# A backbone kernel with latent attention, retention and mLSTM: retention strips moved behind weight copies, an adaLN vector computed in two halves, and separate buffers for the second output projection's input

## The reference

```python
for l in range(DEPTH):
    ml = split(silu(c) @ mod_w[l] + mod_b[l], 6)          # g = 0..5: (l, g) is one vector
    h_lat = x * (1 + ml[1]) + ml[0]
    if l == 0:
        # retention: o = sum_j (q_i . k_j) * decay(i - j) * v_j, in both directions, per head
        ret = head_norm(ret_forward + ret_backward) * silu(rg)
        y = concat([attention, ret]) @ ab_w_out
    else:
        y = (sigmoid(og) * head_norm(h_forward + h_backward) * m_norm_g) @ m_w_out
    x = layer_norm(ALPHA * x + ml[2] * y)
    x = layer_norm(ALPHA * x + ml[5] * swiglu(x * (1 + ml[4]) + ml[3]))
```

## Time and profile before

| | |
|---|---|
| median of 3 runs | 1945.5 us (1937.79, 1945.5, 1948.0) |
| profiled execution | 1948.19 us, its span 1946.3 us |
| mean granted TensorE clock | 0.960 of 2.4 GHz |
| busy: PE, DVE, ACT, POOL | 1796.6 us (92%), 691.5 us (36%), 610.6 us (31%), 724.2 us (37%) |
| DMA | 162.82 MB, mean 84 GB/s |

### The profile page before, as it was taken

How to read it: one execution, slowest core, us unless ns; L and a number is a source line. 1 busy time by engine, 2 the same in 40 slices (tenths; PEclk the granted TensorE clock), 3 DMA queues, 4 the chain that set the end, 5 groups by cost and what they waited for, 6 DMA issues and landing times.

```text
span 1946.3 us, 24417 instructions
## 1 busy us (share of the span) xinstructions
PE 1796.6 (92%) x9832; PEld 1436.2 (74%) x9832; DVE 691.5 (36%) x1183; ACT 610.6 (31%) x859; POOL 724.2 (37%) x381
## 2 busy tenths in 40 slices
PE   4999989999899999999999996989775989999996
PEld 2788757555587888888888883777665878888885
DVE  2134235666467411011111136740078661111114
ACT  1522211555335321122212124442324453132224
POOL 0442200166456423222322245433225664445343
PEclk8999989999999999999999997999877999999998
DMA  8421132255312122122221126212100223323221
GB/s 288 118 55 55 55 119 87 87 174 174 109 55 72 48 65 76 54 65 65 65 65 43 48 62 201 64 56 65 54 1 22 87 70 104 108 87 108 87 78 51
DMA packets 210265, 162.82 MB, mean 84 GB/s; under 512 B 17662, under 2 KB 190942, under 8 KB 210182
## 3 DMA queue, kind: packets, MB, share of 16 engines
q1 hardware_dynamic: 207744, 157.77, 27.3%
q10 hardware_dynamic: 2438, 3.90, 0.5%
HBM read 159.55 MB, written 2.10 MB: 83 GB/s over the span
## 4 chain that ended last, share of the span: by engine, by line
PE 78%; DVE 13%; ACT 4%; issue 2%; DMA 2%; POOL 1%; ACTq 0%; SPq 0%; DVEq 0%
PE ps L662 56%; PE ps L650 2%; PE ps L652 2%; PE ps L651 2%; PE ps L818 2%; PE ps L845 2%; PE ps L870 1%; PE ps L759 1%; PE ps L775 1%; DVE xT L1918 1%; DVE xT L1908 1%; DMA ring<-in_mod_w 1%; PE ps L855 1%; PE ps L604 1%; DVE hlo L1687 1%
## 5 line engine op out<-in xcount | busy, mean ns | idle before, releaser
L2267 POOL TENSOR_TENSOR wsplit<-ring,wsplit 128x1024 fp32r<-128x1024 f32 (+1 forms) x136 | 325.5, 2407 | 531.3 <-ACT wsplit L1405 531.2
L662 PE MATMUL ps<-hhi,wsplit 128*128 128x512 f32 (+1 forms) x1920 | 480.4, 358 | 6.4 <-DVE hu L1965 6.3
L662 PEld LDWEIGHTS ps<-hhi,wsplit 128*128 128x128 f32 x1920 | 316.5, 189 | 61.1 <-DVE hu L1965 6.9
L662 PE MATMUL ps<-hlo,wsplit 128*128 128x512 f32 x960 | 289.9, 356 | 0.0
L662 PE MATMUL ps<-uhi,wsplit 128*128 128x512 f32 x1008 | 253.7, 357 | 0.0
L2015 DVE TENSOR_TENSOR hu<-sg,ps 128x768 f32<-128x768 f32 (+1 forms) x40 | 32.9, 821 | 445.6 <-ACT sg L1474 445.6
L1405 ACT ACTIVATE wsplit<-ring 128x1024 fp32r<-128x1024 f32 (+1 forms) x136 | 135.3, 1025 | 176.0 <-PE ps L662 176.0
L662 PEld LDWEIGHTS ps<-uhi,wsplit 128*128 128x128 f32 x1008 | 165.4, 188 | 27.9
L662 PEld LDWEIGHTS ps<-hlo,wsplit 128*128 128x128 f32 x960 | 160.1, 189 | 29.3
L1881 DVE SCALAR_TENSOR_TENSOR xT<-ps,modc,xT 128x512 f32<-128x512 f32 x96 | 60.6, 659 | 280.5 <-PE ps L662 215.6
L2324 POOL TENSOR_SCALAR lnbuf<-lnbuf,den 128x768 f32<-128x768 f32 (+1 forms) x48 | 85.0, 1778 | 180.3 <-DVE den L1839 179.7
(11 more groups left out here) (326 smaller groups left out, 2737.5 us busy)
## 6 DMA issues: line engine op xcount, KB each, us to landing
ring<-in_mod_w SPq DMA_DIRECT2D x96, 512.0 KB, 4.7
ring<-in_ffn_w_in SPq DMA_DIRECT2D x88, 512.0 KB, 3.8
ring<-in_ffn_w_out SPq DMA_DIRECT2D x32, 512.0 KB, 4.0
ring<-in_m_w_in SPq DMA_DIRECT2D x24, 512.0 KB, 3.6
ring<-in_ab_w_in SPq DMA_DIRECT2D x21, 512.0 KB, 3.9
ring<-in_ffn_w_out SPq DMA_DIRECT2D x16, 384.0 KB, 3.5
ring<-in_ab_w_out SPq DMA_DIRECT2D x8, 512.0 KB, 4.6
ring<-in_m_w_out SPq DMA_DIRECT2D x8, 512.0 KB, 3.8
```

The lines of the kernel that those rows point to most:

```text
L662: mm = pe.matmul(dst[:, a:b], w, h[:, a:b], start=st, stop=sp_)
L2267: pool.tensor_tensor(w_part(s, 1)[:, 0:width], ring[:, (NB[f"ffn{l}"] + s) % RING, 0:width], w_part(s, 0)[:, 0:width].bitcast(F32), ALU.su ...
```

## The change

It joins two changes.

*Strips and vector (0,3).* ACT's `strips(h)` is cut in two: the fourth exponential becomes `strips_end(h)`. For strip 0 one weight copy now stands between the two; strip 1 moves from ahead of the copies NF + 3 to NF + 5 to between the last two copies, with its end behind the last. On PE `mod_rows` of (0,3) is cut after four units (RING); `ret_scores(0)` stands between the halves, and `ret_scores(1)` ahead of the columns. On DVE the last rotation stands ahead of strip 1, the row copies of (0,3) behind weighing 0, its columns behind weighing 1, and `strips_args(2)` behind those.

*Own places.* The rounded chunks go to `oT_a` (chunks 0 to 3), `oT_b` (4, 5) and `oT_c` (6, 7), none of which is read or written under live data; the low parts stay in `hlo_out1`. Each chunk gets a half bank of its own. Chunks 0 to 3 are transposed right behind the last `m_values`, each pair behind its own count of `mn_done`, 4 to 7 in `out_projection`.

```diff
@@ buffers @@
-    hb = under(("hb", [P, LT, D], F32))
+    oT_a, hb = under(("oT_a", [P, KD // 2, LAT], F32R), ("hb", [P, LT, D], F32))
+    _, oT_c = under(("oT_c_pad", [P, KD // 2 * LAT], F32), ("oT_c", [P, 2, LAT], F32R))
...
+    oT_b = sb("oT_b", [P, 2, LAT], F32R, at=ph)
...
+    def out_hi(l, c):
+        return hx[:, 0, c, :] if l == 0 else (oT_a[:, c, :] if c < 4 else (oT_b, oT_c)[c // 2 - 2][:, c % 2, :])
+    def oT_bank(l, c):
+        return op_pair(c) if l == 0 else half(c)
@@ PE @@
-        mod_rows(0, 3, PS[2])
+        mod_rows(0, 3, PS[2], 0, RING)
         ret_scores(0)
+        mod_rows(0, 3, PS[2], RING, KD)
+        ret_scores(1)
         mod_columns(0, 3, PS[2])
-        for h in range(1, H_RET):
+        ret_values(0)
+        for h in range(2, H_RET):
             ret_scores(h)
             ret_values(h - 1)
...
-            for c in rg_chunks(l):
-                if l == 1 and c >= 4:
-                    pe.wait_ge(oT_ev, KD * l + c - 3)
-                if l == 1 and c < 2:
-                    pe.wait_ge(mn_done, NP - 1 + c)
-                if l == 1 and c == 2:
+            for c in (rg_chunks(0) if l == 0 else range(4, KD)):
+                if l == 1 and c == 4:
                     pe.wait_ge(m_num, LT * NP)
+                if l == 1 and c % 2 == 0:
+                    pe.wait_ge(mn_done, c // 2 + 1)
...
+                turn_chunk(l, c, source)
             for m in range(KD):
                 if m < 4:
-                    pe.wait_ge(oT_ev, KD * l + 5 + m)
+                    pe.wait_ge(oT_ev, KD * l + (5 + m if l == 0 else 2 * m + 1))
...
             m_values(i + 3)
+            if p == NP:
+                for c in range(4):
+                    if c % 2 == 0:
+                        pe.wait_ge(mn_done, c // 2 + 1)
+                    turn_chunk(1, c, m_source)
@@ ACT @@
         strips(0)
         split_high("in0", NF + 2, wsp_in0[:, 0])
-        strips(1)
+        strips_end(0)
         for i in range(NF + 3, NF + 6):
             split_high("in0", i, wsp_in0[:, 0])
...
-        for i in range(NF + 6, N_IN0):
-            split_high("in0", i, wsp_in0[:, 0])
+        split_high("in0", NF + 6, wsp_in0[:, 0])
+        strips(1)
+        split_high("in0", NF + 7, wsp_in0[:, 0])
+        strips_end(1)
...
         strips(2)
+        strips_end(2)
         ret_copy(0)
         strips(3)
+        strips_end(3)
@@ DVE @@
-        for h in range(2):
-            strips_args(h)
-            strips_mask(h)
-            strips_sum(h)
+        strips_args(0)
+        strips_mask(0)
+        strips_sum(0)
         rope_ret(8)
-        mod_rows(0, 3, PS[2])
+        strips_args(1)
+        strips_mask(1)
+        strips_sum(1)
...
         ret_weigh(0)
+        mod_rows(0, 3, PS[2])
+        ret_weigh(1)
+        mod_columns(0, 3, PS[2])
         strips_args(2)
-        mod_columns(0, 3, PS[2])
-        ret_weigh(1)
```

More of the change, by code:

```diff
@@ L892, in _, with turn_chunk, m_source, out_projection @@
                     mod_columns(*ATT_MODS[q], half(7))
-        def out_projection(l, source, h_hi, h_lo, wsp):
-            for c in rg_chunks(l):
-                if l == 1 and c >= 4:
-                    pe.wait_ge(oT_ev, KD * l + c - 3)
-                if l == 1 and c < 2:
-                    pe.wait_ge(mn_done, NP - 1 + c)
-                if l == 1 and c == 2:
+        def turn_chunk(l, c, source):
+            for t in range(NT[l] // P):
+                mm = pe.transpose(oT_bank(l, c)[:, t * P:(t + 1) * P], source(c, t), ident)
+            mm.then_inc(oT_mm, 1)
+        def m_source(c, t):
+            return mo[:, t, c * P:(c + 1) * P]
+        def out_projection(l, source, h_lo, wsp):
+            for c in (rg_chunks(0) if l == 0 else range(4, KD)):
+                if l == 1 and c == 4:
                     pe.wait_ge(m_num, LT * NP)
+                if l == 1 and c % 2 == 0:
+                    pe.wait_ge(mn_done, c // 2 + 1)
                 if l == 0 and c == 7:
                     pe.wait_ge(mod_ev, MOD_AT[ATT_MODS[-1]])
-                for t in range(NT[l] // P):
-                    mm = pe.transpose(op_pair(c)[:, t * P:(t + 1) * P], source(c, t), ident)
-                mm.then_inc(oT_mm, 1)
+                turn_chunk(l, c, source)
             for m in range(KD):
                 if m < 4:
-                    pe.wait_ge(oT_ev, KD * l + 5 + m)
+                    pe.wait_ge(oT_ev, KD * l + (5 + m if l == 0 else 2 * m + 1))
                 else:
@@ L1257, in strips, with strips_end @@
             act.activation(stripb, stripb, ACT.Exp, scale=lgc[:, 1, lgb:lgb + 1]).then_inc(strip_exp, 1)
+        def strips_end(h):
+            lgb = H_RET + h
             act.wait_ge(strip_in, 2 * h + 2)
@@ L1420, in out_projection @@
                 if l == 0:
-                    ins = act.activation(hT[:, c, 0:nt], op_pair(c)[:, 0:nt] if c >= 4 else att[:, c, 0:nt], ACT.Copy)
+                    ins = act.activation(out_hi(l, c)[:, 0:nt], op_pair(c)[:, 0:nt] if c >= 4 else att[:, c, 0:nt], ACT.Copy)
                 else:
-                    ins = act.activation(hT[:, c, 0:nt], op_pair(c)[:, 0:nt], ACT.Copy, scale=vcol[:, V_NG + c:V_NG + c + 1])
+                    ins = act.activation(out_hi(l, c)[:, 0:nt], oT_bank(l, c)[:, 0:nt], ACT.Copy, scale=vcol[:, V_NG + c:V_NG + c + 1])
                 ins.then_inc(oT_hi, 1)
@@ L1506, in ffn @@
             layer_norm(2 * l + 1)
-        out_projection(0, hx[:, 0], wsp_out0[:, 0])
+        out_projection(0, wsp_out0[:, 0])
         ffn(0)
@@ L1617, in _ @@
         m_inverse_std(NP - 1)
-        out_projection(1, hT1, wsp_out1[:, 0])
+        out_projection(1, wsp_out1[:, 0])
         ffn(1)
@@ L2037, in ffn @@
                 layer_norm(3)
-        out_projection(0, hx[:, 0], hx[:, 1])
+        out_projection(0, hx[:, 1])
         ffn(0)
@@ L2228, in _ @@
         gains(2)
-        out_projection(1, hT1, hlo_out1)
+        out_projection(1, hlo_out1)
         ffn(1)
```

14 lines of the change are left out of this document (7 added, 7 removed).

## The result

| | before | changed |
|---|---|---|
| median of 15 runs, us | 1938.5 (1932.0 to 1948.0) | 1926.0 (1916.7 to 1935.4) |
| profiled execution, us | 1948.2 | 1919.4 |
| its span, us, and mean granted clock | 1946.3, 0.960 | 1917.5, 0.967 |

The ratio is 0.9915, with a 95% interval of 0.9896 to 0.9934: 0.85% faster, 12.8 to 20.2 us of 1938.5. The two medians themselves differ by 12.6 us. I had forecast 13.7 us. Of all the runs of this document three took far longer than the rest (7175.6, 9889.8 and 2284.6 us; one without the own places, one with the own places alone, one of before beside them); they count in the medians and are left out of the ratios. The two profiles stand 28.8 us apart, about twice the forecast, so the profiles can't be compared by their ends. I compare by the lead: by how much earlier the same event comes in the changed kernel.

The account below looks back on a forecast made before the run. PE, 78% of the chain that ended last, was taken as the bound. 4.3 + 8.0 - 1.3 + 2.7 = 13.7 us off the 1945.5 us median gave 1931.8, say 1932 us; range 1925 to 1942.

Parts of the forecast that it names:

- term B: Vector (0,3) halved around head 0's scores, so PE scores while the last units land: saves 8.0 us.
- A: First stretch, strips behind weight copies: copies come earlier, PE's stop before 212.64 and its slow matmuls go: saves 4.3 us.
- Rival 3: First stop stays: DVE's masks and GpSimd's low part exclude each other too long, or strip 1 too early; 9.4 saved, 0.08.
- C: Head 2's strip chain, started later behind weighing 1 and the columns, holds PE in head 2's scores: costs 1.3 us.
- D: Second output projection, own places for its input: six chunks transposed and rounded early, projection starts sooner: saves 2.7 us.
- Rival 2: Second projection: DVE's low parts and the clock swallow the early transposes, no gain there; 11.0 us saved, chance 0.08.
- Rival 1: Clock falls in the new wait between head 0's and head 1's scores: 2.5 us less, 11.2 saved, chance 0.16.
- Rival 4: Clock stays down through the retention after three PE pauses: slower, 1975 us in the worst case, chance 0.03.
- rival 5: Nothing changes: another engine paces the attention behind the change and takes back the lead; chance 0.03.

Follow-up runs that it names:

- the strips alone: Only the strips moved behind weight copies, the vector (0,3) left whole and no own places, against the kernel before: 1941.9 us, ratio 0.9976.
- the cut at five units: The changed kernel with five units of the vector ahead of head 0's scores and three behind, instead of four and four: 1929.8 us in one execution.
- the three mended orders: Changed kernel with head 2's strip arguments earlier, GpSimd's low parts held, gains ahead of `mrstd`: 1919.4 us, again 1917.1; ratios to before 0.9902, 0.9863.

## Why the prediction was right, and where not

**The whole.** The forecast of 13.7 us saved lies in the measured 12.8 to 20.2, and the median of 1926 us in the range, at its lower edge, 6 us under the 1932 that I had stated. The step that failed is the last one, from the profiled time to the stated one: "the median of the three runs is 1945.5, so I state **1931.8, say 1932 us**". I had taken the three runs' spread for scatter around their middle. Before's fifteen runs lie in two groups, eight from 1932.0 to 1938.5 and seven from 1944.4 to 1948.0; two of my three were of the slow one, and the median of the fifteen is 1938.5. From there 13.7 less is 1924.8. The second step that failed is the size of term B, below. Behind the terms I had also let everything else follow with one pace ("Behind both, PE is the chain again and everything, weights included, follows it"), and the runs showed 9.8 us between two paces of the first FFN. That 13.7 lies so near the 12.6 between the medians is in part luck: the traces show 15.8 us for the terms.

**A, 4.3 forecast.** Right: 4.3 with the strips alone. The unit ended at 218.5 (forecast 218.3), the stop of the rv copies moved and didn't go (220.83), strip 1 was hidden. Of its two halves only the second strip's move counts, which my working didn't separate. The lock cost what I had priced and no more: L1777 took 3.17 us beside GpSimd, and GpSimd was done at 198.3 with PE beginning that unit at 202.1. Rival 3 falls.

**B, 8.0 forecast.** The mechanism was right, the size off: 9.5. The step that failed is the landing of the last unit, "The last unit lands 4.3 earlier, at 264.9", with the reason "SP issues nothing else in between than before": it takes the landing to stand at a fixed distance behind the first group's start. That distance was 11.4 us before and 9.8 in the changed kernel, so the unit landed near 263.5, 1.4 before my time. SP issues the four loads in 1.75 or 1.76 us, and the last lands 9.8 to 10.0 us behind the first group's start, in ten traces of ten in which PE goes on working; in the four in which it stops these are 3.02 to 3.15 and 10.6 to 11.4. What links the two is open. It is shown as going together, not as cause. And head 0's scores stood 0.28 us for the Silu copies, which I had called ready.

**C, 1.3 forecast.** 1.0. The chain took 10.15 us (10.2 forecast), from 271.14 to 281.29; head 2's scores took 7.0 us instead of 6.0, and moving the arguments took the stop away.

**D, 2.7 forecast.** 3.0 at the first unit's end. Transposes 1.97 us for eight; the projection began 1.62 behind them (1.9 forecast). But it hangs on when the clock rises: with the same code at this place the first unit came 9.22 to 9.36 us behind the product in five profiles, and 10.79 in a sixth, which leaves 1.4. Rival 2 falls.

**Rival 1** did not come, as in the changed kernel PE never stood between the two bursts; where the cut at five units made it stand for 2.72 us, the clock fell. My argument against it, that the clock had held through the stop at 222.55 to 224.92, would not have carried: 2.4 us is the distance of two starts there, and the row itself counts 1.35 us of idle time. The stop ahead of 212.64, behind which the clock read 0.50, has 2.38. **Rival 4** (the clock stays down) falls by the windows, and **rival 5** by the lead, 12.2 to 12.6 at the MLA projections and 14.1 at the attention's end.

The local sum is 4.3 + 9.5 - 1.0 + 3.0 = 15.8 us, inside the interval. What stays open: that the three mended orders gained 7 us or more by the medians where the trace shows 2.6 to 4. Ten of their twelve runs are at 1922 or below, and five of the 23 of the changed kernel; even with 4 us allowed for, only eleven of the 23 are at 1926 or below. Whether the kernels draw the fast paces equally often, these few runs can't show.

## What to carry to other kernels

Hide a late transfer behind work that needs nothing of it, and cut exactly where the buffered part ends: one unit further cost 4.1 us, of it 1.7 through the clock. When an operation of DVE takes several times its twin's time, look at what GpSimd runs beside it, and move DVE's critical work or GpSimd's, but then see which DVE operation is next in line. And judge a change of under 1% by the lead at fixed events of two traces, in its own stretch, before looking at medians.

## What was unexpected

- A whole loop has two paces at the same granted clock of 1.00: six matmuls of the first FFN in 1.060 or in 1.040 us, some 527 or 517 us in all. It changed between executions of the same kernel.
- The issue of four 512 KB loads on SP took 3.02 to 3.15 us while PE stood at the landing of one of them, 1.75 or 1.76 while it worked.
- One GpSimd operation of 2.3 us held up the DVE operation that came next, even one of 128x8 elements (2.28 and 2.31 us instead of 0.16). The Trainium skill, "SBUF — State Buffer", section "SBUF: two separate sides", says that only DVE operations with two SBUF inputs or in a two-port mode take that lock; the trace agrees, since the gains have two SBUF inputs, and the low parts with a PSUM input passed beside it at 0.66 us each.
- The same code gave its first finished unit 9.2 or 10.8 us behind the product; in the slower one the clock rose later.
